# Dilated attention encoder on eight cores: score groups issued in twos, reordered first loads and first transposes, and another order of the last tile

## The chip, the cores and the metric

The kernel runs on all 8 cores of one Trainium2 chip. Every core works on its own 4096 tokens with a halo of 1024 tokens on either side, and no core talks to another. The metric is the device time of the slowest core in microseconds (us).

## What is computed

One layer of a hybrid encoder. Cut to what matters:

```python
hn = rmsnorm(x, norm_g)                       # D_MODEL = 1024
proj = hn @ w_in                              # 1024 x 9216
q, k, v, z_a, hc, gb, gc, z_b, g = split(proj)
# mixer A: 3 groups (dilation 1, 4, 16), 8 heads of 64 each; a query sees 64 keys per side, by stride
for gi in range(3):
    out[gi], lse[gi] = dilated_band_attention(q[gi], k[gi], v[gi], DILATIONS[gi], 64, slopes[gi])
attn = sum(softmax(lse over groups) * out)    # [tokens, 512]
a = (silu(z_a) * attn) @ w_attn_out
# mixer B: u = gc * hc, centred depthwise convolution of width 3
c = (silu(z_b) * (gb * conv3(u))) @ w_conv_out
# merge, output projection, residual, final norm
g_a, g_c = split(sigmoid(g + b_gate))
y = rmsnorm(x + (g_a * a + g_c * c) @ w_o, final_g)
```

The scores are exponentiated without a maximum, the distance bias is a multiply by a table of exponentials (zero outside the window), and numerators and denominators of the three groups are added up before one division.

## The kernel before

Matmuls are bf16 with sums in PSUM (8 banks of 512 float columns). Every operation goes through `op`, `pe_group` or `dma`, which work out the semaphore waits from what is read and written; each engine runs its list strictly in the order in which the Python code emits it. So the order of emission is the schedule.

**First stage** (lines 405 to 600). 48 tiles of 128 tokens are loaded by SP's queue (L, six buffers), squared and summed on ScalarE with the statistic on GpSimd (S), normalised on VectorE (N), transposed by TensorE into bank 6 or 7 (T) and copied to the resident tensor `hnT` (E). The functions for the first nine tiles are called by hand through `pipe`. Between them stand `load_consts` (constants; VectorE operations that read `cfp` are emitted in it) and `conv_wload`, the casting DMAs of the convolution's weights on GpSimd's queue. `conv_step` makes 512 tokens of one convolution channel tile: four projections (hc, gc, z_b, gb) of 8 matmuls of 512 columns through `proj_fm` (line 403), with gating on ScalarE and VectorE. In the first step `mid` (behind z_b) and `mid2` (behind gb) hold the transposes of tiles 4 to 7, and tile 8's stand behind the step.

**Attention** (lines 603 to 1059). 24 units: 4 head pairs x 2 halves of the tokens x 3 groups in the order dilation 4, 16, 1. A unit has 8 items of 256 queries for two heads. In an item `stage_a` makes the scores of both heads into banks 2 and 3 (line 807: 6 or 8 matmuls with 64 rows each, one head on rows 0 to 63, the other on rows 64 to 127), ScalarE exponentiates (817), VectorE multiplies by the table (821). `stage_b` multiplies by V with a block of ones (847: full array, 1024 columns), alternately into banks 6 and 7, and adds the result to the accumulator (VectorE 862; in the dilation 4 units ScalarE's copy through 393). While a unit's items run, the pieces of `proj_pieces` make Q, K and V of the next unit (403, 696, 716; copied out by ScalarE 393 for Q and K, VectorE 396 for V) in a ring of the four banks 0, 1, 4, 5. A unit's first piece (`start_piece`) reloads the K and V overlap from DRAM or presets V's ones. In the loop item i emits scores i, then values i-1, then its share of the pieces; a unit's last value group stands behind the next unit's first scores.

After every second item of a dilation 1 unit, `fin_add` queues four parts of finalising 512 tokens, one per item from the next on: copies of the denominators (ScalarE), a reciprocal of 256 columns (VectorE 897) with the gate product (403, tanh 882, gate multiply 886), the second reciprocal, and three products (914, 917, 920) with a store.

In the last unit the pieces are eight gate products of the merge stage, and `c_weights_1` loads w_ao and w_co into the space of unit 22's Q, K and V by GpSimd's queue, emitted behind the last value group of unit 22 (in item 0).

**Merge and output** (lines 1062 to 1205). Eight chunks of 512 tokens: 8 merge steps each (gates 403, products 1078, VectorE 1083 and 1086) and, one chunk behind, four output tiles (1108; residual 1112; square 414; statistic 417, 419; last scaling 1157; store). The last tile (`out_last`) goes by halves of 512 columns: product 1130, sum 1134, square 1137, GpSimd 1140 to 1144, scaling 1148, and tile 30's `out_fin` is emitted ahead of it.

## Time and profile before

| | us |
|---|---|
| median of three runs (lowest, highest) | 1541.97 (1538.83, 1619.25) |
| the profiled execution's own time | 1538.82 |
| its span on the slowest core (core 4) | 1537.3 |
| spans of the eight cores | 1533.4 to 1537.3 |
| TensorE busy on core 4 | 1487.3 |
| VectorE, ScalarE, GpSimd busy | 940.9, 703.1, 142.8 |

The profile covers one execution. A row of the time line or of the chain begins with its start and its length in us from the span's start. Busy times of matmuls overlap, as they are pipelined: the pace of a group is read from one start to the next. "PE" is TensorE, "PEld" its weight loads, "DVE" VectorE, "ACT" ScalarE, "POOL" GpSimd, "SPq" the DMA queue of SyncE. L403 is line 403 of the kernel.

### The profile page before, as it was taken

The numbers are of one execution on the slowest core, as the hardware profiler recorded it, in microseconds if no ns is written. First come the engines' busy times: TensorE is split into PE (matmuls) and PEld (weight loads), VectorE is DVE, ScalarE is ACT, GpSimd is POOL, SyncE is SP. The second block draws the span as 40 slices with busy tenths as digits, with TensorE's granted clock in tenths as the row PEclk, the third lists the DMA queues.
The fourth block names the chain that finished last, engine by engine and source line by source line (L and its number), as shares of the span: only waits on it lengthen the run. The fifth ranks groups of instructions, "written<-read, shape, count | busy, mean of one in ns | idle before, by whom it ended". The sixth has DMA issues, their size and how long they took to land.

```text
span 1537.3 us, 28178 instructions; the slowest of 8 cores (1533.4 to 1537.3 us)
## 1 busy us (share of the span) xinstructions
PE 1487.3 (97%) x11208; PEld 839.4 (55%) x11360; DVE 940.9 (61%) x1476; ACT 703.1 (46%) x1170; POOL 142.8 (9%) x287
## 2 busy tenths in 40 slices
PE   4999999999999999999999999999999999999997
PEld 2454445576566565666866664666444444444443
DVE  4677777235765857567558575685854444444445
ACT  4445544334574656645356557565422222222222
POOL 4212222000010000000000000001100000000001
PEclk9999999999999999999999999999999999999999
DMA  9874545313151422403315205143943222233133
GB/s 244 156 129 101 114 100 88 60 42 79 36 97 15 99 53 52 65 15 64 93 32 102 29 22 105 26 92 50 179 123 110 83 94 98 83 110 108 58 110 124
DMA packets 67764, 132.07 MB, mean 86 GB/s; under 512 B 8752, under 2 KB 34480, under 8 KB 67376
## 3 DMA queue, kind: packets, MB, share of 16 engines
q1 hardware_dynamic: 49296, 96.70, 22.3%
q0 software_dynamic: 18336, 33.56, 15.9%
q8 instruction: 89, 1.46, 0.4%
q14 instruction: 43, 0.35, 0.1%
HBM read 130.17 MB, written 33.62 MB: 107 GB/s over the span
## 4 chain that ended last, share of the span: by engine, by line
PE 85%; DVE 7%; DMA 3%; ACT 2%; issue 2%; SPq 0%; POOL 0%; DVEq 0%; POOLq 0%; ACTq 0%
PE ps L403 49%; PE ps L696 8%; PE ps L1078 7%; PE ps L1108 7%; PE ps L847 5%; PE ps L716 4%; PE ps L807 3%; DVE X L897 2%; DMA X<-w_co 2%; PE ps L448 1%; ACT X L393 1%; DMA gc_s<-X 1%; DVE X L821 1%; DMA X<-xw 1%; ACT X L817 1%
## 5 line engine op out<-in xcount | busy, mean ns | idle before, releaser
L403 PE MATMUL ps<-hnT,wbf 128*128 128x512 bf16 (+1 forms) x2904 | 651.3, 374 | 10.7 <-issue 3.2
L403 PEld LDWEIGHTS ps<-hnT,wbf 128*128 128x128 bf16 x3008 | 281.2, 98 | 313.8 <-issue 8.4
L393 ACT ACTIVATE X<-ps 128x512 bf16<-128x512 f32 (+2 forms) x320 | 219.0, 694 | 206.4 <-PE ps L403 198.2
L821 DVE TENSOR_TENSOR X<-X,et 128x512 bf16<-128x512 bf16 x384 | 159.0, 422 | 217.2 <-ACT X L817 207.9
L817 ACT ACTIVATE X<-ps 128x512 bf16<-128x512 f32 x384 | 207.8, 596 | 148.7 <-PE ps L807 142.6
L403 PE MATMUL ps<-hnT,X 128*128 128x512 bf16 (+1 forms) x1126 | 243.3, 367 | 1.4
L1083 DVE SCALAR_TENSOR_TENSOR hnT<-hnT,ps 128x512 f32<-128x512 f32 x128 | 87.1, 685 | 147.0 <-PE ps L1078 147.0
L403 PEld LDWEIGHTS ps<-hnT,X 128*128 128x128 bf16 x1152 | 107.9, 98 | 125.4 <-DMA X<-w_in 0.4
L696 PE MATMUL ps<-wbf,hnT 128*128 128x128 bf16 x2720 | 164.7, 220 | 0.0
L696 PEld LDWEIGHTS ps<-wbf,hnT 128*128 128x128 bf16 x2720 | 158.5, 114 | 0.2
L978 ACT ACTIVATE hnT<-ps,cf 128x512 f32<-128x512 f32 x128 | 87.4, 683 | 140.4 <-PE ps L403 124.5
L396 DVE CAST X<-ps 128x512 bf16<-128x512 f32 (+2 forms) x152 | 82.9, 565 | 69.7 <-PE ps L696 42.0
L1078 PE MATMUL ps<-X 128*128 128x512 bf16 x500 | 119.8, 379 | 3.5 <-DMA X<-w_co 2.9
L163 POOL DMA_DIRECT2D wbf<-w_in x95 | 51.1, 543 | 762.7 <-PE ps L403 326.9
L414 ACT ACTIVATE et<-X 128x1024 bf16<-128x1024 f32 x40 | 42.2, 1055 | 174.2 <-DVE X L1112 174.1
L847 PE MATMUL ps<-X 128*128 128x128 bf16 (+1 forms) x1280 | 118.2, 231 | 2.9 <-DVE X L821 2.9
L897 DVE RECIPROCAL X<-X 128x256 f32<-128x256 f32 x64 | 111.7, 1745 | 0.0
L1108 PE MATMUL ps<-X,hnT 128*128 128x512 bf16 x487 | 111.0, 379 | 0.5
L862 DVE TENSOR_TENSOR X<-ps,X 128x512 f32<-128x512 f32 x128 | 109.9, 859 | 0.1
L847 PEld LDWEIGHTS ps<-X 128*128 128x128 bf16 x1280 | 84.8, 98 | 36.5 <-issue 11.5
L1078 PEld LDWEIGHTS ps<-X 128*128 128x128 bf16 x512 | 50.0, 98 | 63.3 <-issue 3.4
L1108 PEld LDWEIGHTS ps<-X,hnT 128*128 128x128 bf16 x496 | 48.5, 98 | 58.6
(61 smaller groups left out, 994.8 us busy)
## 6 DMA issues: line engine op xcount, KB each, us to landing
X<-xw SPq DMA_DIRECT2D x80, 512.0 KB, 5.6
wbf<-w_in POOLq DMA_DIRECT2D x95, 256.0 KB, 5.9
y<-X SPq DMA_DIRECT2D x31, 512.0 KB, 2.9
X<-w_in POOLq DMA_DIRECT2D x17, 256.0 KB, 21.0
ga_s<-X SPq DMA_DIRECT2D x32, 128.0 KB, 3.0
X<-ga_s SPq DMA_DIRECT2D x8, 512.0 KB, 6.5
X<-gc_s SPq DMA_DIRECT2D x8, 512.0 KB, 7.0
gc_s<-X SPq DMA_DIRECT2D x24, 128.0 KB, 5.7
```

The costliest lines, as they stand in the source:

```text
L393: return op("act", lambda e: e.activation(out=out, in_=in_, func=AF.Copy), reads=reads, writes=writes)
L403: fns.append(lambda e, kt=kt: e.matmul(bv.cols(c0, n), lhsT=wf(kt), rhs=hnT.cols(kt * WT + t0, n), start=(kt == 0), stop=(kt == 7)))
L696: fns.append(lambda e, tt=tt, kk=kk, p0=p0: e.matmul(bv.cols(tt * 128, 128), lhsT=hnT.ap(kk * WT + p0, [[d, 128]]), rhs=wf(kk), start=(kk ...
L817: op("act", lambda e, bv=bv, hh=hh: e.activation(out=prv.cols(hh * 512, 512), in_=bv.cols(0, 512), func=AF.Exp, scale=0.125), reads=[R_ban ...
L821: op("dve", lambda e, hh=hh, eoff=eoff: e.tensor_tensor(out=prv.ap(hh * 512, [[256, 2], [1, 256]]), in0=prv.ap(hh * 512, [[256, 2], [1, 25 ...
L847: fns.append(lambda e, tk=tk, po=po, oo=oo, n=n, st_=st_, sp_=sp_, hh=hh: e.matmul(bv.cols(hh * 256 + oo, n), lhsT=vb.v.cols(tk * VB_T + 6 ...
L862: op("dve", lambda e: e.tensor_tensor(out=av, in0=ov, in1=av, op=ALU.add), reads=[R_bank[ob]] + ares, writes=ares)
L897: op("dve", lambda e: e.reciprocal(out=rsc.v.cols(256 * q, 256), in_=rsc.v.cols(256 * q, 256)), reads=rsc.r, writes=rsc.r)
L978: op("act", lambda e: e.activation(out=t.v.base, in_=bank(bk).cols(0, 512), func=AF.Tanh, bias=cf.cols(CF_HB + 8 * j + dt_, 1), scale=0.5) ...
L1078: fns.append(lambda e, ct=ct, wv=wv, gv=gv, bv=bv: e.matmul(bv.cols(0, 512), lhsT=wv.v.cols(ct * D + dt_ * 128, 128), rhs=gv.v.cols(ct * 5 ...
L1083: op("dve", lambda e, t=t, bv=bv: e.scalar_tensor_tensor(out=t.v.base, in0=t.v.base, scalar=1.0, in1=bv.cols(0, 512), op0=ALU.add, op1=ALU ...
L1108: fns.append(lambda e, dt_=dt_, nh=nh, bv=bv: e.matmul(bv.cols(0, 512), lhsT=hnT.cols(dt_ * WT + m * 512 + r * 128, 128), rhs=wo_[dt_].v.c ...
```

## The change

Scores: `stage_a` is split into `stage_a` (score matmuls), `stage_e` (exps) and `stage_m` (table multiplies). Even items emit the scores of items i and i+1, then the exps of i; each item emits the value group of item i-2 and then its own multiplies, even items then the exps of i+1. Scores alternate between banks 2-3 and 4-5, all value groups use bank 6, projections the ring 0, 1, 7. `start_piece` stands behind the four Q pieces. The last unit's weight loads are emitted in item 1, its last gate product between the last two value groups. Head: tile 1's load and gvec go ahead of cfp; the first step's transposes of tiles 4 and 5 stand behind gc, 6 and 7 behind z_b, 8 behind gb; tile 7's copy goes to VectorE; the second channel tile's weights are loaded at tiles 7 and 8. Tail: tile 30's step stands behind the last tile's squares; the scale 1/1024 goes into the squares and the sum of the two halves into one operation.

```diff
@@ -337,6 +337,8 @@
             dma("sp", "d_c", View(cbf_t[:]).base, cbf_d.ap(), writes=[R_cbf])
+            first[1][LS]()
+            dma("sp", "d_gb", gb_.v.base, bass.AP(gvec, 0, [[D, 128], [1, D]]), writes=R_gb)
             dma("sp", "d_c2", cf.cols(CF_CW, 32), cfp_d.ap(), writes=[R_const])
@@ -450,7 +452,7 @@
             def E():
-                cp = dve_copy if (i < 5 and i % 2) else act_copy
+                cp = dve_copy if i in (1, 3, 7) else act_copy
                 cp(hnT.ap(ti * 128, [[WT, 8], [1, 128]]), bank_bf(bk).ap(0, [[128, 8], [1, 128]]),
@@ -496,7 +498,7 @@
 
-        def conv_step(ct, c, mid=None, mid2=None):
+        def conv_step(ct, c, mid0=None, mid=None, mid2=None):
             k = cstep["i"] % 2
@@ -517,6 +519,8 @@
                                                 op=ALU.mult), reads=[R_bank[b_gc]] + hcs.r, writes=U.r)
+            if mid0 is not None:
+                mid0()
             proj_fm(b_zb, w_zb, s, 512)
@@ -559,8 +563,7 @@
         load_consts()
-        dma("sp", "d_gb", gb_.v.base, bass.AP(gvec, 0, [[D, 128], [1, D]]), writes=R_gb)
-        pipe([(LS, i) for i in range(1, 6)])
+        pipe([(LS, i) for i in range(2, 6)])
         pipe([(SS, 0), (SS, 1), (NS, 0), (TS, 0)])
@@ -571,8 +574,8 @@
             pipe([(SS, i), (NS, i)])
-            if i < 8:
-                conv_wload(1, (), ((0, 1), (2,), (3,))[i - 5])
+            if i > 6:
+                conv_wload(1, (), ((0, 1), (2, 3))[i - 7])
         conv_wload(2)
@@ -581,8 +584,8 @@
                         conv_step(ct, c, lambda: pipe([(TS, 4), (TS, 5), (ES, 4), (ES, 5)]),
-                                  lambda: pipe([(TS, 6), (TS, 7), (ES, 6), (ES, 7)]))
-                        pipe([(TS, 8), (ES, 8)])
+                                  lambda: pipe([(TS, 6), (TS, 7), (ES, 6), (ES, 7)]),
+                                  lambda: pipe([(TS, 8), (ES, 8)]))
                         stepi += 1
@@ -599,7 +602,7 @@
         pbank = {"i": 0}
-        pb_ring = {"r": (0, 1, 4, 5)}
+        pb_ring = {"r": (0, 1, 7)}
 
@@ -645,7 +648,6 @@
                    reads=[R_patt], writes=vsub(e0, nov))
-            pieces.append((0, start_piece))
 
@@ -662,6 +664,7 @@
                 pieces.append((512, qpiece))
+            pieces.append((0, start_piece))
             ks = k_start(g, h)
@@ -763,7 +766,6 @@
 
-        obank = {"i": 0}
         prc = {"i": 0}
@@ -786,13 +788,12 @@
                     st = {}
-
-                    def stage_a(quad=quad, j=j, st=st):
+                    sb_ = 2 + 2 * (len(items) % 2)
+
+                    def stage_a(quad=quad, j=j, st=st, sb_=sb_):
                         pslot = prc["i"] % 3
...
                         st["pslot"] = pslot
-                        prv = pr_[pslot].v
-                        sb_ = 2
                         fns = []
@@ -811,12 +812,20 @@
                         pe_group(fns, reads=kres + qt.r, writes=[R_bank[sb_], R_bank[sb_ + 1]])
+
+                    def stage_e(st=st, sb_=sb_):
+                        pslot = st["pslot"]
+                        prv = pr_[pslot].v
                         for hh in range(2):
-                            bv = bank(sb_ + hh)
+                            op("act", lambda e, bv=bank(sb_ + hh), hh=hh: e.activation(
+                                out=prv.cols(hh * 512, 512), in_=bv.cols(0, 512), func=AF.Exp, scale=0.125),
+                               reads=[R_bank[sb_ + hh]], writes=xg(65536 + 2048 * pslot + 1024 * hh, 1024))
+
+                    def stage_m(st=st):
+                        pslot = st["pslot"]
+                        prv = pr_[pslot].v
+                        for hh in range(2):
                             pres = xg(65536 + 2048 * pslot + 1024 * hh, 1024)
-                            op("act", lambda e, bv=bv, hh=hh: e.activation(
-                                out=prv.cols(hh * 512, 512), in_=bv.cols(0, 512), func=AF.Exp, scale=0.125),
-                               reads=[R_bank[sb_ + hh]], writes=pres)
                             eoff = es_ * 1536 + (g * 2 + hh) * 256
@@ -827,8 +836,7 @@
                         prv = pr_[pslot].v
-                        ob = 6 + (obank["i"] % 2)
-                        obank["i"] += 1
+                        ob = 6
                         bv = bank(ob)
@@ -861,7 +869,7 @@
                            reads=[R_bank[ob]] + ares, writes=ares)
-                    items.append((stage_a, stage_b))
+                    items.append((stage_a, stage_e, stage_m, stage_b))
             return items
@@ -1002,7 +1010,7 @@
 
-        prev_b = [None]
+        pend = []
         nu = len(units)
@@ -1028,35 +1036,38 @@
 
-            def do_b(ib):
-                items[ib][1]()
-                if g == 0 and ib % 2 == 1 and ib < nit - 1:
+            def do_b(ib, items=items, g=g, hp=hp, h=h):
+                items[ib][3]()
+                if g == 0 and ib % 2 == 1:
                     fin_add(hp, h, ib // 2)
...
             for i in range(nit):
-                items[i][0]()
+                if i % 2 == 0:
+                    items[i][0]()
+                    items[i + 1][0]()
+                    items[i][1]()
+                if len(pend) > 1:
+                    pend.pop(0)()
+                items[i][2]()
+                if i % 2 == 0:
+                    items[i + 1][1]()
+                pend.append(lambda ib=i, do_b=do_b: do_b(ib))
                 fin_run()
-                if i == 0 and prev_b[0] is not None:
-                    prev_b[0]()
-                    prev_b[0] = None
-                    if last_unit:
-                        c_weights_1()
-                        c_weights_2(range(3))
-                        load_chunk(0)
-                if i >= 1:
-                    do_b(i - 1)
+                if last_unit and i == 1:
+                    c_weights_1()
+                    c_weights_2(range(3))
+                    load_chunk(0)
                 while pi < len(nxt) and (i == nit - 1 or spent < total * (i + 1) / nit):
+                    assert i > 0 or nxt[pi][0] == 512
+                    if last_unit and pi + 1 == len(nxt):
+                        break
                     spent += nxt[pi][0]
...
                 gi[0] += 1
-
-            def last_b(items=items, g=g, hp=hp, h=h):
-                items[nit - 1][1]()
-                if g == 0:
-                    fin_add(hp, h, 3)
-            prev_b[0] = last_b
-        prev_b[0]()
+        pend.pop(0)()
+        nxt[-1][1]()
+        pend.pop(0)()
 
@@ -1114,7 +1125,7 @@
 
-        def out_last(i, b0):
+        def out_last(i, b0, between):
             c, r = divmod(i, 4)
@@ -1135,12 +1146,11 @@
                 op("act", lambda e, xh=xh, nh=nh: e.activation(out=junk_.v.cols(512 * nh, 512), in_=xh, func=AF.Square,
-                                                               accum_out=stat.cols(c0 + nh, 1)),
+                                                               scale=1.0 / 32, accum_out=stat.cols(c0 + nh, 1)),
                    reads=xhr, writes=junk_.r + [R_st])
-            op("pool", lambda e: e.tensor_tensor(out=stat.cols(c0, 1), in0=stat.cols(c0, 1), in1=stat.cols(c0 + 1, 1),
-                                                 op=ALU.add), reads=[R_st], writes=[R_st])
-            op("pool", lambda e: e.tensor_scalar(out=stat.cols(c0 + 1, 1), in0=stat.cols(c0, 1), scalar1=1.0 / D,
-                                                 scalar2=EPS, op0=ALU.mult, op1=ALU.add), reads=[R_st], writes=[R_st])
+            between()
+            op("pool", lambda e: e.tensor_scalar(out=stat.cols(c0 + 1, 1), in0=stat.cols(c0, 1), scalar1=stat.cols(c0 + 1, 1),
+                                                 scalar2=EPS, op0=ALU.add, op1=ALU.add), reads=[R_st], writes=[R_st])
             op("pool", lambda e: e.tensor_tensor(out=stat.cols(c0 + 2, 1), in0=stat.cols(c0 + 1, 1),
@@ -1199,8 +1209,7 @@
             out_tick((b0, 6, (b0 + 2) % 6)[k])
-        out_fin(done["fin"])
-        out_last(31, (b0 + 4) % 6)
+        out_last(31, (b0 + 4) % 6, lambda: out_fin(done["fin"]))
```

## Rows read from the trace of the kernel before

**Rows 1.** The page, busy time of TensorE (share of the span)

```profile
PE 1487.3 (97%) x11208; PEld 839.4 (55%) x11360; DVE 940.9 (61%) x1476; ACT 703.1 (46%) x1170; POOL 142.8 (9%) x287
```

**Rows 2.** Waits of TensorE: us in total, times, longest

```profile
PE ps L448 <- DVE X L440: 17.9, 5, 11.8
...
PE ps L847 <- DVE X L821: 2.9, 7, 0.6
```

**Rows 3.** Time line of TensorE, 603 to 609 us: start, length, what

```profile
603.43 3.62 PE L403 MATMUL ps<-hnT,wbf 128*128 128x512 bf16 x16
606.98 0.39 PE L807 MATMUL ps<-X 64*128 64x128 bf16 x6
607.31 0.61 PE L847 MATMUL ps<-X 128*128 128x256 bf16 x6
607.76 1.89 PE L403 MATMUL ps<-hnT,wbf 128*128 128x512 bf16 x8
```

**Rows 4.** Chain that ended last, merge stage: start, length

```profile
1139.28 3.45 PE ps L403 x16
```

**Rows 5.** Time line of TensorE, 1056 to 1122 us

```profile
1066.83 0.62 PE L847 MATMUL ps<-X 128*128 128x128 bf16 x8
...
1095.06 1.02 PE L1078 MATMUL ps<-X 128*128 128x512 bf16 x4 [2.91 <-DMA X<-w_co]
```

**Rows 6.** Chain that ended last, from w_co's issue to its landing

```profile
1069.23 25.69 DMA X<-w_co
```

**Rows 7.** Busy by stretch: length, PE (x), PEld, DVE, ACT, POOL, clock, DMA

```profile
595.00:620.00 25.00, 23.91 (x226) 14.34 (x226) 24.40 (x37) 15.64 (x27) 2.65 (x5) 1.00 0.54 110
```

**Rows 8.** Time line of TensorE and VectorE, 599 to 610 us

```profile
599.33 0.68 DVE L862 TENSOR_TENSOR X<-ps,X 128x512 f32<-128x512 f32 x1
599.93 1.28 DVE L396 CAST X<-ps 128x512 bf16<-128x512 f32 x2
...
601.48 1.67 PE L403 MATMUL ps<-hnT,wbf 128*128 128x512 bf16 x7 [0.16 <-issue]
...
604.59 0.75 DVE L821 TENSOR_TENSOR X<-X,et 128x512 bf16<-128x512 bf16 x2
...
607.37 1.75 DVE L897 RECIPROCAL X<-X 128x256 f32<-128x256 f32 x1
...
609.03 0.63 DVE L886 SCALAR_TENSOR_TENSOR X<-X,ps 128x512 f32<-128x512 f32 x1
```

**Rows 9.** The page, DMA issues: count, KB each, us to landing

```profile
X<-v_s SPq DMA_DIRECT2D x2, 1536.0 KB, 9.6
```

**Rows 10.** Chain that ended last, head: the third x tile's load

```profile
3.39 10.59 DMA X<-xw
```

**Rows 11.** Time line of the head

```profile
10.40 1.28 DVE L440 SCALAR_TENSOR_TENSOR X<-X,stat 128x1024 bf16<-128x1024 f32 x1 [0.34 <-DMA X<-gvec]
...
36.76 13.54 PE L403 MATMUL ps<-hnT,wbf 128*128 128x512 bf16 x61 [1.43 <-ACT hnT L393]
```

**Rows 12.** Time line of the tail

```profile
1522.44 3.62 PE L1130 MATMUL ps<-X,hnT 128*128 128x512 bf16 x15
...
1526.55 1.28 DVE L1157 SCALAR_TENSOR_TENSOR X<-X,stat,et 128x1024 f32<-128x1024 f32 x1 [1.29 <-POOL stat L419]
1527.75 1.28 DVE L1134 SCALAR_TENSOR_TENSOR X<-ps,X 128x512 f32<-128x512 f32 x2
...
1529.45 0.63 ACT L1137 ACTIVATE et<-X 128x512 bf16<-128x512 f32 x1
...
1530.31 0.19 POOL L1140 TENSOR_TENSOR stat<-stat 128x1 f32<-128x1 f32 x1 [3.79 <-ACT et L1137]
1530.59 0.19 POOL L1142 TENSOR_SCALAR stat<-stat 128x1 f32<-128x1 f32 x1
...
1531.45 1.41 DVE L1148 SCALAR_TENSOR_TENSOR X<-X,stat,et 128x512 f32<-128x512 f32 x2 [2.42 <-POOL stat L1144]
```

**Rows 13.** Busy by stretch, core 0: columns as in rows 7

```profile
35.30:38.50 3.20, 3.20 (x9) 1.09 (x8) 2.11 (x5) 0.00 (x0) 0.00 (x0) 0.50 1.01 264
```

## The prediction

> **What bounds the kernel now.** First the page's first part: TensorE is busy in 97% of the 1537.3 us span [rows 1], and its clock stands at full speed over nearly all of it. So only two things can shorten the run: less TensorE time per piece of work, or less idle time at the ends. Next, who TensorE waits for: the head (17.9 us in five waits on the normalised tiles) and 2.9 us in seven waits on VectorE's mask multiply, 0.6 us the longest [rows 2]. Then the time line of TensorE inside the attention, start to start, because busy time overlaps between pipelined matmuls. In [rows 3], two projection groups (16 matmuls of 512 columns) last from 603.43 to 606.98 = 3.55 us when score matmuls follow. The same 16 take 3.45 in the chain where full-array matmuls follow [rows 4]. So going over to the 64-row score matmuls costs about 0.10. A score group lasts 0.33 us (606.98 to 607.31). Its two halves of 64 rows run side by side and stream 512 columns each; the value group behind it streams 1024 columns in 0.45 (607.31 to 607.76), so 512 columns are worth 0.22 to 0.23 and about 0.10 is again extra, the way back. I take 0.095 for each way, readings to the hundredth allowing 0.09 to 0.105.
>
> **Part by part.**
>
> *Score groups of two.* There are 24 units of 8 items, so 192 entries into the 64-row form and 192 exits. With the scores of items i and i+1 issued together there are 96 of each. Each pair saves 2 x 0.095 = 0.19 us. Matmuls, columns, exps, multiplies and copies stay as many as before. 23 units of 4 pairs: 92 x 0.19 = 17.5 us; the last unit's 0.8 ends in front of a DMA wait (below). What hides nothing is TensorE itself, so this comes off the span wherever TensorE is the bound. The seam between the two score groups isn't in this trace. From below: inside a group, equal steps already follow each other on the same row halves within its 0.33, so 0; from above: it costs a full entry, 0.10, and half of the gain is gone. I take 0, as it is the same kind of instruction on both sides.
>
> *The Trainium skill, page "TensorE: Matmul & The Clock Gate", section "The mechanism", says that a weight load overlaps matmuls in flight only when it goes to other row groups. Read strictly, the first load of the second score group would not be hidden, and the pairing would give half: that is the first rival. Against it stands the score group of [rows 3], six matmuls on two row groups, each with its own load, in 0.33 us.*
>
> *Weights of the merge stage.* The DMA of w_co is released by the last value group of unit 22, which today starts at 1066.83 right behind the first scores of unit 23; it is issued at 1069.23, lands 25.69 us later [rows 6], and TensorE waits 2.91 us for it at 1095.06 [rows 5]. Now that value group comes one item later. Counted from the end of unit 22's last projection (T = 1066.50, 0.33 before that start; now 0.45 less because value group 6 moves behind it): two score groups 0.56, value group 6 0.45, gate product 1.73, value group 7 0.45, so it ends at T + 2.74 instead of T + 0.78, 1.96 later. The first of the two big DMAs (w_ao, one issue of 0.8 before w_co) went out some 0.9 us after that release, behind earlier weight loads on POOL's queue, so the issue slips by 1.96 - 0.9 = 1.1. If the queue's transfers are still backlogged then, the landing does not slip, and is even 0.45 earlier in TensorE's work. Bounds -0.45 and +1.1; I take +0.3. TensorE arrives 0.8 earlier, so the wait should read about 4 us on this core (3.2 to 4.8). At the very end value group 7 must wait for value group 6's add (one output bank instead of two) behind a 1.75 us reciprocal: up to 0.7 us, in front of that same DMA wait, so free.
>
> *VectorE's full stretches.* Around each dilation-1 unit the finalising work fills VectorE: 24.40 of 25 us busy at 595 to 620 [rows 7]. Per two items it has two adds (0.68), two pairs of multiplies (0.75), two reciprocals (1.75), one gate multiply (0.63) and three products of about an add's length: 9.1 us, plus 0.64 to 0.68 for each V cast [rows 8]. TensorE needs 0.56 + 0.90 + 1.73 for the gate + 3 x 1.73 = 8.4 us for the same two. So VectorE falls behind there by 0.7 to 2.7 us per pair, up to about 4, and what TensorE gains is limited by how far it may run ahead. Two things change. The value group follows its mask by one more item, but needs the previous add out of the only bank 6: about one item of VectorE work more is asked (4 us less the multiplies), against one item of TensorE time more, which leaves about 0.5 us more room. The projection ring shrinks from four banks to three. Today a gate product begun about 601.3 gives its bank back when the gate multiply ends at 609.66 [rows 8], while the third product behind it starts at 607.76 [rows 3]: with three banks in the old order 1.9 us of stall. In the new order the multiplies and the add stand ahead of the reciprocal; walking the two queues with the durations above, the third product behind the gate comes 1.0 us too early in the second pair, and some 0.3 us of lag from before it. That is 1.3 us where 0.6 stands now, in the four stretches after first halves (12 projection groups per unit); after second halves (14) I find none. 4 x 0.7 = +2.8 us. Bounds: 0, and +6 (the 0.76 us saved by four pairs is all lost in eight stretches).
>
> *Copies and moved pieces.* The unit's start piece (K and V reloads from DRAM on SP's queue, a memset, a pattern copy) goes behind the four Q projections, 1 to 2 items later. Its readers are in the next unit, five items or more away, over 15 us; the largest reload lands in 9.6 us [rows 9]. Cost 0. Scores alternate between banks 2-3 and 4-5, so scores no longer wait for the exps just before: at most the short waits of that kind, 0.
>
> *Head.* SP issues the same bytes ahead of the third x tile, which sets the chain (its landing at 13.98 starts it [rows 10]); so the start of the first projections stays. The second tile comes earlier, but gvec and cfp later, by one 512 KB load, some 1.9 us; the constants' operations on VectorE, which wait for cfp, stand ahead of the first normalisation, which now waits for gvec until 10.40 [rows 11] and moves to about 12.9, and its transposes end just when ScalarE would copy them: +0.25. On the other side TensorE idles 1.43 us before 36.76, waiting for the last transposed tile [rows 11]. With the transposes one product earlier that copy starts at about 35.0 and ends at 36.05, so the second step starts 0.65 sooner. POOL's weight loads for the second channel tile are issued two tiles later; their first use is two steps behind: 0. Sum -0.4, bounds -1.5 and +1.
>
> *Tail.* The last tile's second sum today starts at 1528.34 (half of the pair begun at 1527.75), since VectorE first does the whole output step of tile 30 at 1526.55, itself late for its statistic. TensorE's last matmul ends at 1522.44 + 3.62 = 1526.06 [rows 12]. Now the second sum starts at about 1526.1 and ends at 1526.8; the square ends at 1527.6 with its accumulator, POOL does one short operation fewer (0.28 between the starts of the two), and the last scaling can start at about 1528.7 instead of 1531.45. Tile 30's step (1.27 us) fits in between. -2.75, bounds -2 and -3.2.
>
> Sum: -17.5 + 0.3 + 2.8 - 0.4 - 2.75 = -17.6. The profiled execution took 1538.82 us (span 1537.3 and 1.5 around it), so 1521.2: I say **1521**. That execution is as fast as the lowest run shown and 3 us under their median, so a median of the new kernel may well read 1524.
>
> **Rivals.**
> 1. *The seam costs an entry.* 92 x 0.10 = 9 us come back: 1530. For it: any change of row group at a group's start could act like the entry. Against: [rows 3]. 8%.
> 2. *VectorE takes it all* in its full stretches, in all eight: 8 x (0.76 saved and lost + 0.35, half of the 0.7 above) = 8.9 us instead of 2.8: 1527. For: 98% busy. Against: the value groups have more room. 16%.
> 3. *Slower: the ring of three banks.* Mechanism: a gate product's bank is held until VectorE passes the reciprocal, and every third product stands behind it. There are 32 gate products. At the 1.9 us of today's order each, 61 us less the 2.8 counted: 1579. It decides against the change from (17.6 + 2.8) / 32 = 0.64 us per gate product. For: the hold of 8 us above. Against: TensorE then waits, VectorE catches up, and only a third of the gates lie where VectorE is far behind. 8%, half of it beyond 2%.
> 4. *The clock falls at the longer w_co wait.* Core 0 ran from 35.3 to 38.5 us at half its clock (0.50, the 1.2 GHz level) [rows 13], after TensorE had waited for tiles; none of the present waits at w_co led to that. If some 4 us of idle does, 3 to 7 us at half clock give back 1.7 to 3.5: 1524. *The Trainium skill, same page, section "Why this matters for your kernels", warns of just this: idle gaps between bursts bring the clock back down.* 13%.
>
> The forecast has 55%, own range 1515 to 1526. A measurement of this kernel can tell about 2% (31 us) from no change. All that could go is 18.3 of switches, 3 of tail, 3 of mask waits, 3 of w_co: under 28, so faster by over 2% gets 3%; slower by over 2% 4%; within 93%. Range for 8 in 10: 1514 to 1531, which takes in rivals 1, 2 and 4.
>
> **What would show it.** Two score groups in a row in about 0.55 us, one entry and one exit per pair; score matmul waits gone; a wait at w_co of about 4 us; waits of projections or gates for VectorE of about 1 us in four places; the last scaling 2.7 us after the last matmul instead of 5.4; the step at 36.76 at 36.1. Wrong if the seam shows 0.10 more, if projections wait at many gates, or if value groups wait for bank 6.

## The result and the profile after

| | before | after |
|---|---|---|
| median | 1538.8 us | 1516.7 us |
| ratio of the two, 95% interval | | 0.9851 (0.9829 to 0.9873) |
| the profiled execution, its span | 1538.8, 1537.3 | 1517.5, 1515.9 |

In some executions the cores of one die ran at a lower granted clock (1619.25 us before, 1744.08 after); the medians and ratios here leave these out.

The change makes the kernel 1.5% faster, 21 to 23 us. The forecast was 1521 in 1514 to 1531, and "within 2%", which is what came. The saving forecast, 17.6 us, was some 4 us short, and several terms behind it were wrong while their errors partly cancelled. Read from the time lines of all eight cores (middle values, us; a "merge matmul" is one of line 1078 before and 1089 after):

| stretch | before | after | forecast |
|---|---|---|---|
| start of the first score matmul | 296.2 | 296.1 | -0.4 |
| from there to the last value group | 794.2 | 775.9 | -18.3 + 2.8 |
| first to thirteenth merge matmul | 8.4 | 8.3 | +1.1 |
| from there to the last matmul's end | 424.1 | 424.1 | 0 |
| last matmul's end to the span's end | 11.2 | 9.0 | -2.75 |

Of the 4 us that the forecast lacks, the attention gives 2.8 and the merge's start 1.3; head and tail give 0.9 less than forecast. The slowest core's span fell by 21.4 us and the middle one by 20.3 (1534.4 to 1514.1): before, core 4 was slowest, with its 2.91 us wait at w_co of [rows 5], which none of the eight cores has now. The page of after, and the waits of TensorE on its slowest core (core 7), which answer to [rows 1, 2]:

```profile
PE 1477.8 (97%) x11360; PEld 848.1 (56%) x11360; DVE 927.4 (61%) x1477; ACT 697.8 (46%) x1169; POOL 141.5 (9%) x286
```

```profile
PE ps L450 <- DVE X L442: 18.5, 5, 14.0
PE ps L719 <- DVE X L398: 2.1, 1, 2.1
PE ps L855 <- DVE X L870: 1.6, 2, 1.1
PE ps L405 <- DVE hnT L398: 1.6, 1, 1.6
PE ps L808 <- ACT X L395: 1.5, 2, 0.8
...
PE ps L1089 <- DMA X<-gc_s: 0.5, 1, 0.5
```

The seven waits for the mask multiply (2.9 us) are gone. New are one wait of 2.1 us (a V product, L719), two for the output bank's add (L870, 1.6 us), and one for gc_s instead of w_co.

**The pair of score groups.** Time line of TensorE after, answering to [rows 3]:

```profile
592.09 0.62 PE L808 MATMUL ps<-X 64*128 64x128 bf16 x12
592.64 0.61 PE L855 MATMUL ps<-X 128*128 128x256 bf16 x6
593.09 3.62 PE L405 MATMUL ps<-hnT,wbf 128*128 128x512 bf16 x16
596.54 0.60 PE L855 MATMUL ps<-X 128*128 128x256 bf16 x6
596.99 3.62 PE L405 MATMUL ps<-hnT,wbf 128*128 128x512 bf16 x16
```

Two groups of six take 0.55 us (592.09 to 592.64), one took 0.33: the second adds 0.22, what 512 columns take in a value group. The seam costs nothing that can be read here, and the second item has no switch at all: its 16 projection matmuls and nothing else fill 593.09 to 596.54 = 3.45 us. Rival 1 has fallen with this row. The Trainium skill's sentence in "TensorE: Matmul & The Clock Gate", section "The mechanism", that a weight load overlaps matmuls only on other row groups, does not bind at this seam: the second group's 0.22 us hold its own six loads.

**VectorE.** The group of the mask multiply on the page, before and after; the last figures are VectorE's idle time just before it and its releaser:

```profile
L821 DVE TENSOR_TENSOR X<-X,et 128x512 bf16<-128x512 bf16 x384 | 159.0, 422 | 217.2 <-ACT X L817 207.9
L862 DVE TENSOR_TENSOR X<-ps,X 128x512 f32<-128x512 f32 x128 | 109.9, 859 | 0.1
```

```profile
L830 DVE TENSOR_TENSOR X<-X,et 128x512 bf16<-128x512 bf16 x384 | 145.9, 419 | 37.3 <-ACT X L820 36.3
L870 DVE TENSOR_TENSOR X<-ps,X 128x512 f32<-128x512 f32 x128 | 110.9, 866 | 157.9 <-PE ps L855 118.5
```

VectorE used to stand 208 us in all before its multiplies, waiting for exps; now 36. Over the whole kernel this is no gain of room: its idle time before the adds (the second line of each pair) went from 0.1 to 157.9 us. What counts is the full stretches. The one of [rows 7] has eight reciprocals between 585.8 and 621.2 us, and near its start VectorE idles once, for the exps of the next item:

```profile
590.71 0.92 DVE L821 TENSOR_TENSOR X<-X,et 128x512 bf16<-128x512 bf16 x2 [1.98 <-ACT X L817]
```

After the change this hole is gone: the same stretch runs from 580.7 to 614.2, 33.5 us instead of 35.3. Within it VectorE is as busy as in [rows 7], with no wait of TensorE in 25 us:

```profile
585.00:610.00 25.00, 25.00 (x235) 15.41 (x233) 24.49 (x38) 16.24 (x29) 2.13 (x5) 1.00 0.35 83
```

**The new wait.** The chain at 715 us, then the time line of VectorE, TensorE and GpSimd there:

```profile
715.32 8.54 DMA v_s<-X
```

```profile
711.24 3.17 POOL L163 DMA_DIRECT2D wbf<-w_in  x6 [59.24 <-PE ps L405]
...
723.88 0.76 DVE L398 CAST X<-ps 128x256 bf16<-128x256 f32 x2 [4.05 <-DMA v_s<-X]
...
724.37 3.42 PE L719 MATMUL ps<-wbf,hnT 128*128 128x256 bf16 x16 [2.11 <-DVE X L398]
```

In this unit every V product is also staged for a store to DRAM, in two buffers of 96 KB. Six casting weight loads go out at 711.24, the store at 715.32 lands 8.54 us later, the next cast waits for the buffer, and TensorE for the cast. Before, five of the weight loads went out from 715.55 and the first of these stores only at 727.86. Now the last gate product of the unit before runs an item later (it ends 1.7 us ahead of the V products instead of 9.9), so its slot and those behind it come free just as the stores begin. On cores 1 and 7 the clock fell right behind this wait. Busy by stretch on core 7 (the figure ahead of the last two is the granted clock):

```profile
724.80:728.00 3.20, 3.20 (x18) 2.46 (x16) 0.76 (x2) 0.00 (x0) 0.00 (x0) 0.50 0.22 63
728.20:731.20 3.00, 3.00 (x31) 3.00 (x29) 2.05 (x6) 1.16 (x1) 0.00 (x0) 1.00 0.20 66
```

At 0.50, the 1.2 GHz level, 18 matmuls fit in 3.2 us; at full clock 31 in 3.0. By these two rows I estimate 1.5 us more on these cores. Their attention lasts 776.6 us, that of the other six 775.4 to 777.1 (middle 775.8), so in the length of the stretch less than that can be seen.

**The last unit, the head and the tail.** GpSimd's and SP's issues in the last unit after:

```profile
1049.39 0.77 POOL L163 DMA_DIRECT2D X<-w_ao  x1 [0.17 <-issue]
1050.19 0.75 POOL L163 DMA_DIRECT2D X<-w_co  x1
```

```profile
1051.41 0.52 SPq L163 DMA_DIRECT2D X<-gc_s  x1
```

Before, gc_s went out ahead of w_ao (1068.43) and w_co (1069.23):

```profile
1068.05 0.40 SPq L163 DMA_DIRECT2D X<-gc_s  x1
```

TensorE after, from the last unit to the merge's start, then at the step after the head, then the tail:

```profile
1047.46 0.62 PE L808 MATMUL ps<-X 64*128 64x128 bf16 x12
...
1050.19 0.61 PE L855 MATMUL ps<-X 128*128 128x128 bf16 x8
...
1069.70 0.60 PE L855 MATMUL ps<-X 128*128 128x256 bf16 x6 [0.47 <-DVE X L870]
...
1073.17 0.60 PE L855 MATMUL ps<-X 128*128 128x256 bf16 x6 [1.14 <-DVE X L870]
...
1075.09 1.04 PE L1089 MATMUL ps<-X 128*128 128x512 bf16 x4 [0.46 <-DMA X<-gc_s]
```

```profile
36.05 4.26 PE L405 MATMUL ps<-hnT,wbf 128*128 128x512 bf16 x19 [0.83 <-ACT X L395]
```

```profile
1502.45 3.62 PE L1141 MATMUL ps<-X,hnT 128*128 128x512 bf16 x16
...
1506.53 1.28 DVE L1145 SCALAR_TENSOR_TENSOR X<-ps,X 128x512 f32<-128x512 f32 x2
...
1510.11 1.42 DVE L1158 SCALAR_TENSOR_TENSOR X<-X,stat,et 128x512 f32<-128x512 f32 x2 [1.06 <-POOL stat L1154]
```

w_co is issued 2.73 us after the last unit's first scores (1047.46 to 1050.19), as before (1066.50 to 1069.23), and w_ao goes out ahead of value group 7's start at 1050.19. So these DMAs were never released by that value group. The ones that are, are ga_s and gc_s. With value group 7 an item later, gc_s is now issued behind the two 1 MB loads w_ao and w_co instead of ahead of them, and by core it lands 22.8 to 24.8 us after its issue instead of 15.9 to 18.2. On five cores TensorE waits for it (0.2 to 1.6 us), and on the other three it lands less than 0.3 us before TensorE comes.

The step after the head starts at 36.05 on this core, near the forecast 36.1. That it was forecast rightly can't be said: over the eight cores its start is 35.7 to 36.6 (middle 36.1) now, and was 35.1 to 36.8 (middle 35.8) before; the forecast set out from core 4's 36.76. The wait before it is down from 1.2 or 1.4 us to 0.8 or 1.0, and its releaser is no longer the last transposed tile. In the tail the last scaling follows the last matmul's end (1506.07) by 4.0 us instead of 5.4 on this core, where 2.7 was forecast; on cores 3 and 5 it is 2.8.

### The profile page after: what moved, and what is told of

Same layout as the page of the kernel before. It is cut to its first block, busy times and chain, and to the rows that moved or that the text cites. A ratio compares the mean times of both kernels' runs of the same rounds, so it can differ in the third digit from the quotient of the medians.

```text
span 1515.9 us, 28477 instructions; the slowest of 8 cores (1511.9 to 1515.9 us)
## 1 busy us (share of the span) xinstructions
PE 1477.8 (97%) x11360; PEld 848.1 (56%) x11360; DVE 927.4 (61%) x1477; ACT 697.8 (46%) x1169; POOL 141.5 (9%) x286
## 4 chain that ended last, share of the span: by engine, by line
PE 90%; DMA 6%; DVE 3%; issue 1%; ACT 0%; SPq 0%; POOL 0%; DVEq 0%; POOLq 0%; ACTq 0%
PE ps L405 52%; PE ps L699 10%; PE ps L1089 7%; PE ps L1119 6%; PE ps L855 6%; PE ps L719 3%; PE ps L808 3%; DMA X<-xw 2%; DMA gc_s<-X 2%; DMA X<-gc_s 2%; PE ps L450 1%; DVE X L905 1%; DMA v_s<-X 1%; DVE X L830 0%; DVE X L442 0%
## 5 line engine op out<-in xcount | busy, mean ns | idle before, releaser
L405 PE MATMUL ps<-hnT,wbf 128*128 128x512 bf16 (+1 forms) x3008 | 665.5, 373 | 2.6 <-DVE hnT L398 1.6
L820 ACT ACTIVATE X<-ps 128x512 bf16<-128x512 f32 x384 | 204.1, 614 | 116.9 <-PE ps L808 116.9
L870 DVE TENSOR_TENSOR X<-ps,X 128x512 f32<-128x512 f32 x128 | 110.9, 866 | 157.9 <-PE ps L855 118.5
L830 DVE TENSOR_TENSOR X<-X,et 128x512 bf16<-128x512 bf16 x384 | 145.9, 419 | 37.3 <-ACT X L820 36.3
L416 ACT ACTIVATE et<-X 128x1024 bf16<-128x1024 f32 x40 | 42.2, 1056 | 174.7 <-DVE X L1123 173.4
L855 PEld LDWEIGHTS ps<-X 128*128 128x128 bf16 x1280 | 89.9, 98 | 36.0 <-issue 10.9
L1089 PEld LDWEIGHTS ps<-X 128*128 128x128 bf16 x512 | 50.0, 98 | 60.9 <-DMA X<-gc_s 0.9
```

What stands on the lines that cost most here:

```text
L405: fns.append(lambda e, kt=kt: e.matmul(bv.cols(c0, n), lhsT=wf(kt), rhs=hnT.cols(kt * WT + t0, n), start=(kt == 0), stop=(kt == 7)))
L820: op("act", lambda e, bv=bank(sb_ + hh), hh=hh: e.activation(out=prv.cols(hh * 512, 512), in_=bv.cols(0, 512), func=AF.Exp, scale=0.125), ...
L830: op("dve", lambda e, hh=hh, eoff=eoff: e.tensor_tensor(out=prv.ap(hh * 512, [[256, 2], [1, 256]]), in0=prv.ap(hh * 512, [[256, 2], [1, 25 ...
L855: fns.append(lambda e, tk=tk, po=po, oo=oo, n=n, st_=st_, sp_=sp_, hh=hh: e.matmul(bv.cols(hh * 256 + oo, n), lhsT=vb.v.cols(tk * VB_T + 6 ...
L870: op("dve", lambda e: e.tensor_tensor(out=av, in0=ov, in1=av, op=ALU.add), reads=[R_bank[ob]] + ares, writes=ares)
L1089: fns.append(lambda e, ct=ct, wv=wv, gv=gv, bv=bv: e.matmul(bv.cols(0, 512), lhsT=wv.v.cols(ct * D + dt_ * 128, 128), rhs=gv.v.cols(ct * 5 ...
```

## The experiments

**e1, score groups issued singly again.** Everything else as changed (banks, lag of two items, ring of three, head, tail).

```diff
-                if i % 2 == 0:
-                    items[i][0]()
-                    items[i + 1][0]()
-                    items[i][1]()
+                items[i][0]()
+                items[i][1]()
...
                 items[i][2]()
-                if i % 2 == 0:
-                    items[i + 1][1]()
```

> The changed kernel with its score groups issued singly again, each at its own item; banks, lag of two items, ring of three and everything else as changed. Theory (the gain is the switch of TensorE into and out of the 64-row form): 96 more entries and exits at 0.19 us the pair, so +18 us against the changed kernel (1517 to about 1535), and a time line with 0.33 us per score group. Rival (the gain is the longer distance between scores and values, which hides VectorE): within 3 us of the changed kernel.

Measured: 1539.1 us in the profiled run, 22 us over the changed kernel; the attention (first score matmul to last value group) lasts 798.1 instead of 775.9. 96 entries and exits at 0.19 us are 18.3 of these 22.2 us. Of the rest, the waits for the gate multiply, which the pairs hardly have, are 0.8 to 4.4 us by core (on this core two of 2.9 together, and one of 0.4). The waits for V casts are about as long in the pairs (2.0 to 2.6 us):

```profile
PE ps L405 <- DVE X L894: 2.9, 2, 1.4
PE ps L719 <- DVE X L398: 2.4, 3, 1.5
```

```profile
616.38 0.85 DVE L830 TENSOR_TENSOR X<-X,et 128x512 bf16<-128x512 bf16 x2 [1.48 <-ACT X L820]
...
619.25 1.74 DVE L905 RECIPROCAL X<-X 128x256 f32<-128x256 f32 x1
620.91 0.63 DVE L894 SCALAR_TENSOR_TENSOR X<-X,ps 128x512 f32<-128x512 f32 x1
...
621.60 1.25 PE L405 MATMUL ps<-hnT,wbf 128*128 128x512 bf16 x5 [1.45 <-DVE X L894]
```

This is the stall that the prediction put at 1.3 us in the stretches after first halves: a product that needs the bank of the gate product, behind a reciprocal. It exists, but in the single order. In pairs the second item's exps are done an item early, so VectorE has no hole before its multiplies in such a stretch, and it reaches the gate multiply in time. e1 bears this out within itself: in this stretch VectorE idles 1.48 us for an exp at 616.38 and TensorE then 1.45 us at 621.60, in the one at 399 us 1.80 and 1.45; in those at 809 and 996 us VectorE has no such hole, and there is no stall. Why these two have none stays open.

Over the whole kernel VectorE's idle time before the multiplies is 79.2 us here and 37.3 in pairs, so most of the fall from 217 comes with the lag of two items and the new banks, not with the pairs. Against the kernel before, e1's attention is 3.9 us longer: the banks, the lag and the order alone cost, and the pairs gain more than the net.

**e2, the attention's part alone, and e3, the head's and the tail's alone**, each put on the kernel before. Their diffs are the hunks of the change between lines 599 and 1060, and the others.

> The kernel of before with the attention's part of the change alone (pairs, lag of two, banks, ring, start piece, last unit). Theory: -18 us in the attention and some 1 to 3 more from waits gone, less the new waits of 2.1 and 1.6 us: 1519 to 1521. Rival (head and tail carry more than 3 us): 1523 or more.

> The kernel of before with the head's and the tail's part alone. Theory: tail -2.3, head between -0.7 and +0.3: 1537 to 1538.5, by time hardly told from no change, but the last scaling starts about 4 us after the last matmul instead of 5.4. Rival (head gives 1 us or more): the first scores start below 295.5 us on the middle core.

Measured: e2 0.9888 (0.9868 to 0.9908), 1520.6 us, the attention 775.5; e3 0.9979 (0.9968 to 0.9990), 1534.0 us. The parts add up by these ratios: -17.2 and -3.2 us against -22.9 for both, within the intervals. Last matmul to end of span is 11.2 us before and in e2, 8.6 in e3: the tail gives 2.6. The first scores start at 295.9 in e3 (before 296.2, e2 296.1): the head gives 0.1 to 0.3. In all nine traces with the new head they start at 295.3 to 296.1, in the three with the old one at 295.9 to 296.2.

My range for e3's median missed by 3 us. Part of it is that I set out from too high a time: beside e3 the kernel before has a median of 1537.2, not 1539 to 1542. And the wait at w_co, 2.9 us on core 4 before, differs from run to run; in e3 it is at most 1.4.

With the old head the clock stood at 0.50 for some 3 us between 35 and 41 us in four cores of the kernel before ([rows 13] is one), in four of e2 and in six of e5; with the new head in no core of any trace. Before, the first scores start at 296.2 to 296.6 us in the cores with it and at 296.1 to 296.9 in those without. So the new head's 0.1 to 0.3 us may come from an earlier step or from the clock; no run tells them apart.

**e4, a third staging buffer for the V store.**

```diff
-        vst_ = [xb(81920 + 768 * i, 768, BF16) for i in range(2)]
+        vst_ = [xb(81920 + 768 * i, 768, BF16) for i in range(3)]
...
-                    k = vsc["i"] % 2
+                    k = vsc["i"] % 3
...
-                        vsc["left"] = 2
+                        vsc["left"] = 3
```

> The changed kernel with three staging buffers instead of two for the V store of the dilation-16 units. Theory (TensorE's 2.1 us wait at 722 us is VectorE waiting for a staging buffer whose store lands 8.5 us late, behind six weight loads issued just before): the third buffer gives one more product of 3.5/2 us, the wait falls to under 0.6 us and the time by 1.5 to 2 us, and on cores whose clock fell behind this wait by 1.7 more. Rival (VectorE itself is too slow there): the wait stays at 2 us.

Measured: 1515.2 us, ratio to the kernel before 0.9857 (0.9833 to 0.9881). The attention lasts 774.2 instead of 775.9 (775.3 in e10, the changed kernel once more), and no core's clock falls there. The waits for V casts are 0.6 to 1.5 us in all by core, the longest 0.3 to 1.2; in the changed kernel 2.0 to 2.6 and 1.5 to 2.3. On core 0:

```profile
PE ps L719 <- DVE X L398: 1.1, 2, 0.8
```

So the staging buffer was what TensorE waited for, in the main: "under 0.6" holds for the longest wait on four of the eight cores. In the time of the whole kernel the gain is within its scatter; the stretch shows 1.0 to 1.7 us.

**e5, the shortage of banks in the old order**, and **e6, one bank less in the new order.**

```diff
-        pb_ring = {"r": (0, 1, 4, 5)}
+        pb_ring = {"r": (0, 1, 4)}
...
-                        ob = 6 + (obank["i"] % 2)
+                        ob = 6
```

```diff
-        pb_ring = {"r": (0, 1, 7)}
+        pb_ring = {"r": (0, 1)}
```

> The kernel of before with the changed kernel's shortage of banks alone: projections in a ring of three (0, 1, 4), all value groups in bank 6, order as before. Theory (the three-bank ring would have cost what was forecast, 1.3 us in place of 0.6 in four stretches, and the paired order is what saves it): projections wait 1 to 2 us for the gate multiply in the four stretches at 430, 620, 835 and 1025 us, 3 to 8 us in all. Rival (the forecast overrated the ring in any order): the waits stay as before, below 1 us more.

> The changed kernel with one bank less in the ring of projections (0, 1). Theory (in the paired order VectorE reaches the gate multiply sooner, but a bank is still held 4 us or more): projections now wait for the gate multiply at most of the 32 gates, 15 to 50 us in all. Rival (VectorE is hardly behind in this order): under 10 us.

Measured, one execution each: e5 1559.5 us, 21 us over the kernel before; e6 1535.6, 19 us over the changed one. The waits of TensorE, e5 (core 2) and then e6 (core 0):

```profile
PE ps L847 <- DVE X L862: 21.1, 33, 1.6
...
PE ps L403 <- DVE X L886: 1.6, 2, 1.2
```

```profile
PE ps L405 <- DVE X L894: 15.2, 18, 1.7
PE ps L719 <- DVE X L398: 4.1, 2, 3.4
```

Both my theory and its rival missed e5: the waits at gates are 1.6 us, at 714 and 730 us and not in the four stretches, but the single output bank costs 21.1 us in 33 waits (a value group for the add of the one before). e5 changes two things at once, and a TensorE that waits for the output bank gives VectorE time to catch up; what the ring of three alone costs in the old order, no run shows.

The changed kernel has the same single output bank and waits 1.6 us at two places, e1 with its single score groups 1.4 us. So what makes the difference is not the pairs but where the add stands: in the old order it is emitted behind the multiplies and the finalising parts of its item, and the next value group comes one item on; with the lag of two it is the first thing of the item on VectorE.

e6 confirms that a gate product's bank is held long: with two banks in the ring TensorE waits for the gate multiply 18 times over 32 gates, 11.2 to 15.2 us by core. The theory's 15 to 50 is met on two cores only. e6 also waits 3.8 to 5.0 us for V casts, and on seven cores the clock then stands at 0.50 for 3 to 7 us. All in all it loses 0.6 us per gate and is still 3 us faster than the kernel before: rival 3, which needed 0.64 us per gate, stayed short of that even with one bank less.

**e7, the ends of the last unit loosened** (on e4), and **e8, value group ahead of the first scores where the last K copy is late** (on e7).

```diff
+                    if u == len(units) - 1 and len(items) >= 6:
+                        ob_ = sb_
+                    if u == len(units) - 2 and len(items) == 7:
+                        ob_ = 7
...
                 if len(pend) > 1:
                     pend.pop(0)()
+                    if last_unit and i == 0:
+                        pend.pop(0)()
...
-                if last_unit and i == 1:
+                if last_unit and i == 0:
```

```diff
+                early = i == 0 and g == 2 and h == 0 and hp % 2 == 1
+                if early:
+                    pend.pop(0)()
```

> The kernel of the third staging buffer with the last unit's ends loosened: its last two value groups write the banks of their own scores, and unit 22's last value group follows at once in bank 7, so that the first chunk's loads start 1.7 us earlier. Theory (1.6 us of waits for bank 6 at 1066 and 1069 us stand on the path, and the gc_s wait behind them is a matter of when its load starts): both waits go, -1.6 us, the wait for gc_s stays below 1 us; 1512.5 to 1514 against 1515. Rival (the first chunk's load is bound by the DMA engines): what is saved returns as a wait at gc_s, within 0.5 us of 1515.

> As e7, and in the two dilation-16 units whose last piece is a K product (second and fourth head pair, first half) the older value group is issued ahead of the first scores. Theory (the 0.75 us waits at 531 and 928 us are the last K copy on ScalarE, which the value group's 0.45 us and its switch can cover): 0.9 us less in all than e7. Rival: the exps come later and the value groups behind them wait, no gain.

Measured: e7 1515.1 us (0.9849, 0.9834 to 0.9864), e8 1514.6 (0.9846, 0.9830 to 0.9863); the attention 775.3 and 774.5 against 774.2 in e4. e8 did shorten the two 0.75 us waits (1.5 us in all) to 0.3 each, and its attention is 0.8 us shorter than e7's, as its theory had it. e7 missed its 1512.5 to 1514: it moved its waits, it did not remove them. The rival's time came, but by another way than the rival had it:

```profile
PE ps L405 <- DVE X L875: 2.1, 1, 2.1
...
PE ps L860 <- DVE X L835: 1.2, 1, 1.2
```

Bank 7, given to a value group out of turn, was the next one of the ring, and its add stood behind another add: 2.1 us. And the last value group now waits for its own mask multiply, in front of which a reciprocal and a gate multiply had been emitted. Only the wait for gc_s went.

**e9, both repaired, and e10, the changed kernel again on the same chip.** In e9, on e8, the value group takes the ring's next bank, and the finalising parts are emitted behind the item's multiplies.

```diff
-                        ob = ob_
+                        ob = next_pbank() if ob_ is None else ob_
...
-            fin_run()
+            if tail_[0]:
+                fin_run()
```

> The third staging buffer and e8's order, with two repairs of what e7 showed: unit 22's last value group takes the next bank of the projection ring instead of bank 7 by name, and the finalising parts are emitted behind the item's mask multiplies instead of ahead of them. Theory (the 2 us wait at 1045 us was the bank taken out of turn, and the 1.18 us wait at the last value group was a reciprocal and a gate multiply in front of its mask multiply on VectorE): both waits below 0.5 us, attention some 3 us shorter than with the third buffer alone, 1511 to 1513. Rival (VectorE has no room there whatever its order): the waits only move, 1514 to 1515 again.

> The changed kernel itself once more, on the same chip as e9, as its yardstick: 1516 to 1518, with the wait of about 2 us for the staged V store at 722 us and the two waits for bank 6 at the end of the attention.

Measured: e9 1516.5 us (0.9857, 0.9841 to 0.9872), e10 1516.9 (0.9861, 0.9843 to 0.9878). e9 missed its 1511 to 1513. Its attention is the shortest, 773.6, but only 0.6 us shorter than e4's where 3 was forecast; the waits at the value groups are gone, and six short ones for a gate multiply have come (1.7 us). And the first merge matmuls now take 9.5 us instead of the 8.0 of e10, as they wait for weights: on seven of the eight cores 0.6 to 1.1 us for w_co, on five of them then 0.4 to 2.0 for w_in. On core 5:

```profile
PE ps L405 <- DMA X<-w_in: 2.0, 1, 2.0
PE ps L405 <- DVE X L899: 1.7, 6, 0.7
...
PE ps L1102 <- DMA X<-w_co: 0.6, 1, 0.6
```

In e8 no core waits there. So in e9 the start of the merge is bound by its weight DMAs, and what it saves ahead of them comes back there. No version beats the changed kernel by more than its scatter: e4 and e8 read lowest, by about 2 us, but by their ratios to the kernel before on the same chip, 0.9857 and 0.9846, they can't be told from the changed kernel (0.9851 and 0.9861).

## Why the prediction was right, and where it was wrong

The main term was right. That the sum came within 4 us of the measurement is partly luck, since wrong terms of either sign stand beside it.

- **Score groups of two** (-17.5 and 0.8 in front of a DMA wait): right, in mechanism and size. The seam is 0, there are 96 entries and exits less, and e1 gives them back. That the attention is shorter by just 96 x 0.19 = 18.3 us is partly luck: the pairs against e1 are worth 22.2, the rest of the attention's change costs 3.9, and the mask waits gone (2.9 us) stand against new waits of 2.1 and 1.6. That the last unit's 0.8 us would end in front of a DMA wait was right in form, but the DMA is gc_s and not w_co.
- **VectorE's full stretches** (+2.8): wrong. I forecast four stalls of 1.3 us in place of 0.6. There are none, and the old ones went too. The failing step is the walk of the two queues: it summed VectorE's work and took it as dense. It left out the hole of 1.98 us before the multiplies at 590.71, which stands in each such stretch before and which the pairs close (35.3 us become 33.5); e1, where the hole can stay, has the stall. The mechanism, a gate product's bank held behind a reciprocal, is real: in e1 it costs 0.8 to 4.4 us by core, about what was forecast for the pairs, in e6 11 to 15.
- **The output bank**: "about 0.5 us more room" had the right sign; e5 shows how much hangs on it in the old order, 21 us, which I had not seen at all. It is the lag of two that gives the room, as e1 shows.
- **Weights of the merge stage** (+0.3, a wait of about 4 us): wrong in its first sentence. I took w_co as released by value group 7, because it is emitted behind it. The buffer that it overwrites holds V tiles that earlier value groups read last, so in both kernels it is issued 2.73 us after the unit's first scores. Its landing time differs between cores and runs (before, 25.7 us on core 4 and 21.5 to 23.7 on the others), so the 2.91 us of [rows 5] was no fixed price. gc_s and ga_s are the ones released there; they were not in the sum. TensorE's wait for gc_s is 0.5 us on core 7 and up to 1.6 on others. The steps between, a load released by value group 7 and so issued later, were right for it.
- **Value groups 6 and 7 at the end** ("up to 0.7 us, free"): 1.6 us. It was as good as free, though not in front of w_co: gc_s was issued ahead of these waits and landed after TensorE's arrival or less than 0.3 us before it on all eight cores, so without them TensorE would have waited longer for gc_s. This is read from the times; e7, which was to show it, moved gc_s as well.
- **Copies and moved pieces** (0): the start piece cost nothing, but the wait at 722 us was missed. I looked at readers of moved loads, not at what a gate product one item later does to the weight slots that it frees. The price is 2.1 us; e4 gives 1.0 to 1.7 of it back.
- **Head** (-0.4): 0.1 to 0.3 gained, but not by the step that was forecast: on the middle of the cores it starts no sooner. **Tail** (-2.75): right where its loads land in time. On cores 3 and 5 the last scaling starts 2.8 us behind the last matmul and the tail is 2.6 us shorter, as it is in the middle of e3. On core 7 it is 1.4 shorter: VectorE there waited 3.43 us for an x tile in tile 29's step. The walk left out that wait, which was 1.3 to 2.9 us in the eight cores before and is 2.1 to 4.0 now.
- **The clock** (rival 4): it fell, but behind the wait at 722 us on two cores, not at w_co. Of the Trainium skill's warning ("TensorE: Matmul & The Clock Gate", section "Why this matters for your kernels") that idle gaps bring the clock down, core 7's trace is an instance, with 0.50 for 3.4 us after a wait of 2.1; core 0 waited 2.3 us at the same place and kept its clock.

## What to carry over

When TensorE alternates between matmuls on half of its rows and full ones, count the changes, not the matmuls: here each cost 0.095 us, and issuing two groups together removed half of them for nothing. Before taking a full engine as dense, look at its idle time by releaser, within the full stretch and not over the whole kernel: an order that feeds it an item earlier can close a hole of 2 us there, while the kernel's total of idle time only moves from one operation to another. When a buffer becomes free follows from its last reader, not from the place where the overwriting load is emitted. And a wait is worth only what no later wait would take back: before removing one, look at which load lands just behind it.

## What was not expected of the hardware

A 96 KB store issued 4 us after the first of six weight loads landed in 8.5 us, where the median of such stores is 1.6; that the loads are the cause is read from the order in time, no run takes them away. A double-buffered store that was hardly in the way (0.8 us of VectorE's waits before) became the longest wait of TensorE in the attention. In the same way the 512 KB load gc_s took 16 to 18 us ahead of two 1 MB loads and 23 to 25 behind them. What decides whether a wait of some 2 us lets the clock fall stays open: of eight cores with 1.5 to 2.3 us at the same place, two fell. Of e6's eight cores with 3.4 to 3.7 us, seven fell.
